# A two-block network on one core: weight tiles and scratch moved to the next multiple of 128 bytes

## The reference

```python
# first block: DEPTH = 2 layers
for layer in range(2):
    u = x * (1 + scale) + shift                     # from ada_mod(c)
    y = even_mixer(u) if layer == 0 else fox_attention(u)
    x = layer_norm(ALPHA * x + gate * y)
    u = x * (1 + scale) + shift
    y = square(relu(u @ mlp_w1 + mlp_b1)) @ mlp_w2 + mlp_b2
    x = layer_norm(ALPHA * x + gate * y)
# second block
mix = token_mixing(x)      # w_in, spatial mixing in chunks, causal conv of width 31, w_out
x = layernorm(ALPHA_2 * x + mix)
ffn = (silu(conv3(x @ w_up))[gate] * conv3(x @ w_up)[val]) @ w_down
x = layernorm(ALPHA_2 * x + ffn)
```

## Time and profile before

| | |
|---|---|
| median of 3 runs | 4192.61 us (4184.55 to 4200.64) |
| profiled execution, its time | 4186.48 us |
| profiled execution, its span | 4184.7 us |
| PE busy | 3908.5 us (93%), 18934 matmuls |
| LDWEIGHTS busy | 3168.1 us (76%) |
| DVE, ACT, POOL busy | 49%, 28%, 46% |
| DMA | 224.65 MB, mean 54 GB/s |
| mean granted TensorE clock | 0.968 |

### The profile page before, as it was taken

How to read it: one execution, slowest core, us unless ns; L and a number is a source line. 1 busy time by engine, 2 the same in 40 slices (tenths; PEclk the granted TensorE clock), 3 DMA queues, 4 the chain that set the end, 5 groups by cost and what they waited for, 6 DMA issues and landing times.

```text
span 4184.7 us, 50589 instructions
## 1 busy us (share of the span) xinstructions
PE 3908.5 (93%) x18934; PEld 3168.1 (76%) x18934; DVE 2069.1 (49%) x3073; ACT 1175.8 (28%) x1891; POOL 1918.4 (46%) x748
## 2 busy tenths in 40 slices
PE   6899899999999999999997999999999889999997
PEld 5677777888877777777775777777877667888886
DVE  6864564344354645545546422111479675444445
ACT  5322231111114444444432211111223242222222
POOL 2543286665554322222212774455464475445352
PEclk9999999999999999999988999999999999999999
DMA  6311013223211111011101111111111111111111
GB/s 217 117 56 33 19 51 96 89 88 102 81 46 31 36 36 35 27 31 36 36 21 31 41 56 45 40 45 55 41 35 52 41 51 51 44 46 50 40 60 40
DMA packets 246709, 224.65 MB, mean 54 GB/s; under 512 B 12916, under 2 KB 194834, under 8 KB 246563
## 3 DMA queue, kind: packets, MB, share of 16 engines
q1 hardware_dynamic: 222496, 171.09, 13.5%
q10 hardware_dynamic: 24067, 51.53, 3.8%
HBM read 218.33 MB, written 4.26 MB: 53 GB/s over the span
## 4 chain that ended last, share of the span: by engine, by line
PE 80%; DVE 13%; ACT 3%; issue 2%; DMA 1%; ACTq 0%; SPq 0%; DVEq 0%
PE PS L658 11%; PE PS L660 10%; PE PS L659 10%; PE PS L788 6%; PE PS L790 5%; PE PS L789 5%; PE PS L685 3%; PE PS L687 3%; PE PS L686 3%; PE PS L1143 3%; DVE ADMS L2130 2%; PE PS L1128 1%; PE PS L1113 1%; PE PS L1055 1%; PE PS L1075 1%
## 5 line engine op out<-in xcount | busy, mean ns | idle before, releaser
L3063 POOL TENSOR_SCALAR WH<-RAW 128x1024 fp32r<-128x1024 f32 x255 | 731.9, 2870 | 1293.6 <-PE PS L687 512.0
L658 PE MATMUL PS<-UH,WH 128*128 128x512 f32 (+1 forms) x2192 | 877.8, 400 | 13.4 <-DVE UL L2184 3.5
L659 PE MATMUL PS<-UL,WH 128*128 128x512 f32 (+1 forms) x2192 | 871.0, 397 | 0.0
L660 PE MATMUL PS<-UH,WL 128*128 128x512 f32 (+1 forms) x2192 | 871.0, 397 | 0.0
L3065 POOL TENSOR_TENSOR WL<-RAW,WH 128x1024 fp32r<-128x1024 f32 x255 | 622.7, 2442 | 21.3
L2141 DVE TENSOR_TENSOR X<-PS,X 128x512 f32<-128x512 f32 x432 | 292.7, 687 | 432.5 <-PE PS L790 421.4
L658 PEld LDWEIGHTS PS<-UH,WH 128*128 128x128 f32 (+1 forms) x2192 | 413.5, 189 | 120.0 <-issue 5.9
L660 PEld LDWEIGHTS PS<-UH,WL 128*128 128x128 f32 (+1 forms) x2192 | 412.6, 188 | 103.4
L659 PEld LDWEIGHTS PS<-UL,WH 128*128 128x128 f32 (+1 forms) x2192 | 413.2, 189 | 100.1 <-issue 0.2
L788 PE MATMUL PS<-WH,HH 128*128 128x512 f32 x1024 | 405.6, 396 | 26.2 <-DVE X L2141 13.4
L790 PE MATMUL PS<-WL,HH 128*128 128x512 f32 x1024 | 400.6, 391 | 0.0
(11 more groups left out here) (364 smaller groups left out, 7167.5 us busy)
## 6 DMA issues: line engine op xcount, KB each, us to landing
RAW<-in_mlp_w_dram SPq DMA_DIRECT2D x128, 512.0 KB, 3.9
ADM<-in_ada_w_dram ACTq DMA_DIRECT2D x96, 256.0 KB, 3.2
RAW<-in_w_up_dram SPq DMA_DIRECT2D x44, 512.0 KB, 3.8
ADR<-in_ada_w_dram ACTq DMA_DIRECT2D x32, 512.0 KB, 4.0
RAW<-in_w_down_dram SPq DMA_DIRECT2D x22, 512.0 KB, 3.5
RAW<-in_ev_w_in_dram SPq DMA_DIRECT2D x20, 512.0 KB, 3.9
RAW<-in_w_in_dram SPq DMA_DIRECT2D x20, 512.0 KB, 4.0
ADS<-in_ada_w_dram SPq DMA_DIRECT2D x16, 512.0 KB, 8.9
```

What stands on the lines that cost most here:

```text
L658: pe.matmul(bank(b)[0:width], wh, xh, start=(k == 0), stop=False)
L659: pe.matmul(bank(b)[0:width], wh, xl, start=False, stop=False)
L660: mm = pe.matmul(bank(b)[0:width], wl, xh, start=False, stop=(k == NK - 1))
L3063: pool.tensor_scalar(WH[slot][:, 0:n], r[:, 0:n], 1.0, None, ALU.mult).then_inc(S("w_hi"), 1)
```

## The change

One line rounds o up before the weight tiles and the scratch are placed. BST8 and MV8, whose lines follow it, don't depend on o.

```diff
--- before.py
+++ after.py
@@ -305,6 +305,7 @@
         BF = small("BF", [16, 1])
         IDENTR = small("IDENTR", [P, P], F32R)
         RS = small("RS", [P, NT])
+        o = (o + 127) // 128 * 128
         BST8 = at("BST8", [P, NT, 12], base + 96 * KB + 4 * 656)
         MV8 = at("MV8", [P, NT, 2], base + 96 * KB + 4 * 752)
         WH = [at(f"WH{i}", [P, 1024], o + 8 * KB * i, F32R) for i in range(NSLOT)]
```

## The result

The median of the changed kernel is 4156.65 us (11 runs, 4151.78 to 4180.93) beside 4192.61 us for the kernel before, measured with it; the ratio is 0.9921 [0.9901, 0.994]. The kernel is 36 us faster, on the side forecast and inside the range of 4120 to 4196, and 14 us short of the 4143 named as likeliest. The profiled execution took 4152.71 us; its numbers stand against the earlier trace rows. Each line of the kernel has a number one higher than before, so L658 is now L659.

A forecast was written before the change was run, and what follows sets the result against it. PE, busy in 93% of the span, was taken as the bound: matmul count times start-to-start distance. Gains of 44.2 + 5.5 = 49.7 us off 4186.5 gave 4136.8, plus 6.1 for the median: 4143 us, range 4120 to 4196 (own range 4120 to 4162).

The forecast's parts named there:

- The mechanism: 128x512 matmuls: 0.2267 us start to start when both operands have the same offset, 0.2336 with U against a weight tile.
- Rival 1: 128x512 matmuls: U itself, for instance its place in memory, sorts the levels; no change, 4193 us; chance 0.14.
- rival 2: All 128x512 matmuls: each operand's start at a multiple of 128 is dear; slower, +102, 4295 us; chance 0.07.
- rival 3: All 12576 128x512 matmuls: both starts on the boundary save a further 6.8 ns; 4070 us; chance 0.07.
- The z tile: 16 columns wide, stationary slices stepping 64 bytes: three matmuls take 0.68 or 0.70 us, repeating after 256 bytes; cited as support.
- Step (a): 7680 128x512 matmuls with U on one side: 6.8 ns each, 52.2 us of PE time, 44.2 on the path.
- Step (b): 2304 128x256 matmuls with UL or UH stationary: 3 ns each, 6.9 us, 5.5 on the path; range -16 to +16.
- the 64-wide row: L1143, both operands in the scratch, 0.1114 us a matmul: taken to bound the 128x256 gain at 6.9 ns.
- Steps (c) to (e): 128x512 matmuls with both operands behind the rounding, transposes with IDENT, and the other engines: 0 gain each.
- Rival 4: Gain swallowed in first MLP, even and odd stages, 128x256 matmuls giving nothing: 30 us, 4163 us; chance 0.12.
- the two terms at their ends: Forecast's own range: 128x256 matmuls at -16 or +16 us, 128x512 matmuls with U at 52 or 34 us.
- the list of signs: What would show it right: steps at 0.2267 us, L788 unchanged, both MLPs about 10 us shorter each, FFN 14.

The follow-up runs named there:

- u_32: Changed kernel with X, U and the small tensors 32 bytes further, weight tiles still on the boundary: 4187.54 us, 0.9984 of the kernel before.
- all_96: Changed kernel with U, weight tiles and scratch all at 96 modulo 128 bytes, relation kept: 4156.44 us, 0.99 of the kernel before.
- pairs: Separate small kernel, only matmuls on zeros, stationary start moved line by line: 512 wide 0.2271 us a step equal modulo 256, 0.2333 at 32 apart.
- pairs_fine: pairs at further distances (8 to 252 bytes) and with one low part alone moved: 512 wide 0.2304 us at 176, 0.2267 at 252, none below.
- w_64: Changed kernel with weight tiles and scratch 64 bytes behind the boundary, U on it: 4185.39 us, 0.9984 of the kernel before.
- tok_64: Changed kernel with moving slices of token_item and vg_piece 64 bytes earlier (first quarter 192 later), values not the reference's: 4164.52 us, 0.996 of the kernel before.

## Why the prediction was right, and where it was off

**The mechanism** was the one named. Rival 1 (U's own place) and rival 2 (a dear boundary) fell with u_32, all_96 and pairs, where the same distance gives the same step at both places; rival 3 (a further level below 0.2267) fell with pairs_fine. What the earlier trace rows suggested, a period of 256, holds. What I did not have from them is which distances are good (mod 256, for 512 columns): 32 and 128 apart are bad alike for a wide stationary operand, so a rounding that made U and the weight tiles agree modulo 128 only would have brought nothing. The z tile itself doesn't follow the table of pairs (its k = 0 was 32 short of equal and at 0.2267); pairs has no 16-column stationary operand, and this stays open. The rule of the Trainium skill that was weighed ("SBUF — State Buffer", "Who interferes with whom"), by which PE waits on nobody, would have given no change; the 226.7 against 233.3 ns of pairs, where only an offset differs, speak against drawing that from it.

**Step (a), size per matmul.** 6.8 ns was taken, 6.4 measured in u_item, 5.6 in row_item, 3.7 in the q pieces. The last have a reason that the timelines show: in the changed kernel a q piece of 12 or 24 matmuls begins at some 231 ns a step and reaches 226.7 with about the tenth. And the matmuls at the lower clock gain nothing. The timeline of the kernel before in such a stretch:

```profile
388.98 0.63 PE L659 MATMUL PS<-UL,WH 128*128 128x512 f32 x1
...
390.26 0.63 PE L659 MATMUL PS<-UL,WH 128*128 128x512 f32 x1
```

1.28 / 3 = 0.427 us, with unequal starts; in pairs 0.427 is also the step of the equal first line, while its clock is still low. 273 us of the span before and 277 after are at that level. The Trainium skill ("TensorE: Matmul & The Clock Gate", "Back-to-back issue gap") gives N / 1.2 ns at the low clock, by which 512 columns would take 426.7 ns, an estimate from that page; here the trace agrees with its 0.427 us. PE time gained by this account: 6528 x 6.4 + 384 x 5.6 + 768 x 3.7 = 46.8 us, where 52.2 were taken.

**Step (a), what of it is on the path.** In the column of the second MLP 1440 u_item matmuls went from 233.4 to 226.7 ns, 9.6 us of PE time, and 1533 downs from 227.4 to 227.1, 0.4 us; the stage gave 10.1. In the FFN's it was 1920 x 6.7 = 12.9 us and 0.5 in the out_items, and the stage gave 13.3: where the chain is PE, all of it arrives. In the first MLP a round has 192 u_item matmuls and 192 downs, 1.34 us of PE time gained; 0.48 us went to the longer wait for HL and 0.85 arrived, 63%. The forecast took 59% from the chain's share and named that wait, so this reading held, and 7.5 rounds of 0.85 would be 6.4 us where 5.8 were forecast. That only 3.0 came is the lower clock in two rounds, 3.2 us. So what the sum had wrong here is not the path but the clock: **it kept the clock as it was** and had no term for it, and the longer wait that it named came right before each of those stretches. In the even stage the u_items gained 5.4 ns each, some 4 us with the token_items' loss taken off, and 1.2 came instead of 5.2; no experiment looked at it. In token mixing (768 u_items of 6.1 ns, 4.7 us, and 2.2 of row_items, less 0.6 of narrow ones) 4.4 us came instead of 7.7. The chain by line in 3060:3460, in the kernel before and in the changed one, shows how near another engine was there:

```profile
by line: PE PS L658 11.5%; PE PS L659 11.4%; PE PS L660 11.4%; DVE PS L2712 7.7%; PE PS L1274 6.5%; PE PS L1276 6.2%; PE PS L1275 6.2%; PE PS L673 3.0%; PE PS L674 2.6%; PE PS L675 2.6%; PE PS L715 2.0%; DVE UU L2778 1.7%; PE PS L677 1.7%; 
```

```profile
by line: DVE PS L2713 31.6%; PE PS L1275 6.4%; PE PS L1277 6.2%; PE PS L1276 6.2%; issue 3.9%; PE PS L661 3.9%; PE PS L659 3.9%; PE PS L660 3.9%; DVE FY L2857 2.6%; DVE BSX L2727 2.0%; DVE UU L2779 1.8%; PE PS L716 1.7%; DVE X L2194 1.7%; D
```

L2713, DVE's causal convolution, is 7.7% of the chain before and 31.6% after; in all_96 it is 33.9%, in u_32 and w_64, which have the old step, 7.7%. Windows moved along with the stage give the same (32.1% of 3046:3439 in the changed kernel). So the faster PE made another chain the last; that the two had been within a few us of each other is my reading, and no run tests it. The 85% that I took for this stage had no row; this chain would have been one.

**Step (b) had the wrong sign.** 3 ns gained for each of 2304 matmuls was the middle between "nothing" and the 64-wide row; measured is 1.4 ns lost, 3.2 us of PE time lost where 6.9 gained was taken. The 64-wide row was no neighbour: pairs shows that the good distance depends on the width. The bound below nothing that the range had (-16 us) covered it. With 46.8 - 3.2 = 43.6 us the sum of PE time stands close to the 44.2 of the page.

**Steps (c) to (e)** held: L789 has the durations of L788, PE's longest waits name the same producers in both kernels, and DVE, ACT and POOL are at 2081.9, 1174.9 and 1912.4 us against 2069.1, 1175.8 and 1918.4. Most of DVE's 12.8 us more is HL (133.0 to 144.8 us for 128 of them); their median stays at 0.69 us and it is the long ones that got longer, most of them in the second MLP, where PE doesn't wait for HL. Why was not looked into.

**Rival 4**, the swallowed gain, was no rival but a part of the truth: 49.7 - 34.9 = 14.8 us are missing. Of these (b) accounts for some 8 (5.5 forecast, 2.6 lost, at the 80% taken for it), the short gain of the q pieces for 2 (768 x 3.1 ns, at 86%) and the lower clock in the first MLP for 3; the rest, estimated like these, lies in the even stage and token mixing. In the odd stage the PE time gained was small to begin with: 768 x 3.7 ns = 2.8 us in the q pieces, less 1536 x 1.4 = 2.2 in vg_piece. What of it arrived (-2.4 us, forecast -8.2) can't be told from the scatter of its clock; 959 to 968 us without the relation, 955 to 966 with it.

**The range and the signs.** The measured time is near the upper end of the forecast's own 4120 to 4162. These bounds are not what the two terms at their ends give, some 4125 to 4175 (52 + 16 and 34 - 16 us off 4192.6). And the list of signs had 10 us for each MLP, where the sum had 6.2 for the first.

## What to carry to other kernels

When 128x512 float32r matmuls set the time, place the operands so that the stationary and the moving one start at the same offset modulo 256 bytes, all parts of each; check the 256-wide ones apart, since they want another distance. Read the rate of matmuls as the distance of their starts, over stretches that lie in one clock level, and compare stages only beside the time that each spent at the lower clock. Count a gain per matmul in full only where PE is alone on the chain: elsewhere a part of it turns into longer waits, and in the first MLP here the lower clock came with these and took half of what had arrived (3.2 of 6.4 us).

## What the runs showed of the hardware

- The step of a 128x512 float32r matmul depends on the distance of its operands' starts modulo 256 bytes: settled, 226.7 ns at 0 and at 252, 228.3 at 240, 228.9 at 192, 230.7 at 8, and 230 to 234.1 at the others tried (pairs, pairs_fine). Shifting both by 96 bytes changes nothing.
- A 128x256 matmul prefers other distances: 113.3 ns at 64 and at 88, 120.0 at 0 and at 96, and 117 to 120 elsewhere.
- The first up to ten matmuls of a stretch can be slower than the settled rate, so pieces of 12 see only part of the gain (3.7 of 6.4 ns in the q pieces); two of the equal lines of pairs were settled from the first.
- At the lower clock the distance doesn't matter: 0.427 us either way.
- In the first MLP each of the stretches at the lower clock inside a loop round (3.4 us, 1.6 us lost) began 0.4 to 0.8 us after PE had waited 1.82 us, in the profiles of five kernels; in the five with shorter waits there was none. Not every such wait was followed by one.
- How long the odd stage is granted the lower clock varies between kernels that hardly differ (61 us in the changed kernel, 85 in all_96, 109 in tok_64), and the stage's time with it. An edit worth less than some 10 us in this stage can't be judged by one profile.
